# Expert blocks of a transformer kernel: VectorE's products ahead of the move of the last result, TensorE's turning of the products in two halves

## Chip, cores, metric

The kernel runs on one core of a Trainium2 chip (trn2) in one launch. The metric is device time in microseconds, the median of several runs.

## What is computed

A block of 512 tokens of width 1024 passes through a first layer (a parallel mixer, cross attention and a mixture of experts) and two further layers (a token mixer with four branches, a norm, a mixture of experts, a norm). All in float32. The change is in the mixture of experts, which occurs three times. Cut to what matters:

```python
# 4 groups x 8 experts; top-1 group, then the top-2 experts in it
expert_id = g_idx * EXPERTS_PER_GROUP + e_local            # (T, 2)
weights = p_top * softmax(e_top)
# rows are sorted by expert and padded to blocks; each block has one expert e
def expert_block(xb, e):
    return (silu(xb @ w_gate[e]) * (xb @ w_up[e])) @ w_down[e]
out[t] += w_sorted[t] * y_disp[dest]                       # two contributions a token
```

The first mixture has gate and up matrices of 1024x512 an expert, the second and third of 1024x256. There are 32 experts in each, and 1024 pairs of token and expert.

## The kernel before

`program` calls its stages one after the other, with a barrier of all engines between them. Three calls of `moe` are the expert stages; their tiles have the prefix `e_` in the profile. I call them first (FF = 512), second and third stage (FF = 256).

**Work and tiles.** In `moe` the tokens of each expert are cut into blocks of SLOTS = 64 rows, so that most experts have one block and a few have two or more (some 35 blocks a stage). Gate and up weights lie in a ring of RING places (3 in the first stage, 6 in the others), down weights in another. SyncE fills both at the start; then `refill` loads expert e + RING into a place as soon as the gate and up matmuls of expert e are through (`gu_ready`), and its down weights as soon as its down matmuls are (`y_ready`).

**One block g, by engine.** Every engine has its own loop over experts and their blocks, and counts them in a register `done`. What happens in it is in the order of the code:

- GpSimd gathers the rows of block g + 3 from DRAM into `landing` (`gather`), when `stage_rows` has emptied it. Then it waits for VectorE's `move_y` of block g's result (`y_moved`) and stores `y_out` to DRAM by an indirect DMA (L1223). Both go through the queue for software-made DMAs, with two small operations ahead of each issue (`tokcur` or `choicecur`, and `aside`).
- VectorE: `move_y(g)` copies block g - 1's result from `y` to `y_out` (L1162). It waits for ScalarE's copy to `y` (`y_copied`) and for the store before the last (`y_stored`), which has to have left `y_out`. Then, for each half q, the product of silu(gate) and up into `hid` (L1170); `turn_copy(g + 2)` copies the turned rows of the next block to `xT` (L1140, L1142); `stage_rows(g + 2)` waits for the gather and copies `landing` to `gathered` (L1147).
- TensorE: 2 x 8 pairs of gate and up matmuls, half by half (L997, L999); `turn`, which turns the gathered rows of the next block with the identity matrix (L976, L978); the turning of the products, half 0 and half 1, each after `hid_ready` (L1009); the down matmuls (L1020), which wait for ScalarE's copies `hidT` and for `y_copied`.
- ScalarE: two silus (L1048), two copies of the turned products to `hidT` (L1051), then the copy of the result to `y` (L1055), which waits for `y_moved`: `y` may be overwritten once the last result has been moved.

The waits around the move, in the code:

```python
                def move_y(n):
                    dve.wait_ge(y_copied, n + 1)
                    dve.wait_ge(y_stored, n * 16 + 16)
                    vec.tensor_copy(y_out[:], y[:]).then_inc(y_moved, 1)
```

Before the loops, GpSimd issues two spare stores (L1204), so that `y_stored` is already 32 for the first moves, and gathers 0, 1 and 2. VectorE scales `x` before its first `stage_rows` in the second and third stage (L1151). After the loops VectorE moves the last result; SyncE reads all results back when every store has landed (L941), and VectorE adds them to `x` (L1181).

## Time and profile before

| | us |
|---|---|
| median of 3 runs | 3223.39 |
| lowest, highest | 3221.16, 3237.9 |
| the profiled execution | 3233.42 |
| its span, first to last instruction | 3231.7 |
| busy: TensorE / VectorE / ScalarE / GpSimd | 2530.7 / 1255.3 / 944.7 / 364.4 |
| granted TensorE clock, mean | 0.879 |

How to read the profile. Times are counted from the start of the span. PE is TensorE (PEld its weight loads), DVE VectorE, ACT ScalarE, POOL GpSimd, SP SyncE; a q behind a name is that engine's sequencer. A group or an instruction is named by its line in the kernel, engine, operation, and written tile <- read tiles. In brackets or behind a bar stands the idle time of the engine just before it, and what ended it. A granted clock of 1 is 2.4 GHz and 0.5 is 1.2 GHz. An indirect DMA's row on GpSimd is its issue, not its transfer. The share of DMA is the mean busy share of the core's 16 DMA engines.

### The profile page before, as it was taken

What the parts mean: (1) busy time and instruction counts of PE and PEld (TensorE: products, weight loads), DVE (VectorE), ACT (ScalarE), POOL (GpSimd) and SP (SyncE); (2) the same over time, 40 slices, a digit from 0 to 9 for tenths busy, and PEclk for the clock granted to TensorE, in tenths of its full rate; (3) what the DMA queues carried; (4) which work ended last, traced back from release to release, by engine and by line L of the source; (5) the groups of instructions that cost most, each with busy time, mean ns of one, the idle gap of its engine ahead of it and who ended that gap; (6) DMA issues with size and microseconds to landing.
All of it is one profiled execution on the core that took longest, in us unless ns stands there. A gap on an engine that the chain in (4) does not pass through costs nothing. (4 is left out here: it accounts for less than half of the span.)

```text
span 3231.7 us, 51558 instructions
## 1 busy us (share of the span) xinstructions
PE 2530.7 (78%) x17988; PEld 1959.7 (61%) x17989; DVE 1255.3 (39%) x2672; ACT 944.7 (29%) x1720; POOL 364.4 (11%) x706
## 2 busy tenths in 40 slices
PE   4974698589889859699898388894969998658883
PEld 4963688445445438476677266663847677636662
DVE  3447334311111145447443432235734753432224
ACT  2233323112112122236322133332234532213232
POOL 0000000012111110000000233231000000113233
PEclk9987899789999979799999598896979999768887
DMA  3201231489999942122121669944122121289972
GB/s 119 80 1 39 66 117 53 181 354 407 414 409 412 404 153 75 33 66 66 50 57 56 276 234 348 349 182 139 53 57 58 49 63 44 65 347 363 362 298 100
DMA packets 208903, 565.75 MB, mean 175 GB/s; under 512 B 26198, under 2 KB 170198, under 8 KB 184192
## 3 DMA queue, kind: packets, MB, share of 16 engines
q1 hardware_dynamic: 191056, 538.71, 45.1%
q0 software_dynamic: 17712, 25.23, 2.4%
q8 instruction: 86, 1.41, 0.2%
q14 instruction: 49, 0.40, 0.0%
HBM read 560.18 MB, written 35.92 MB: 184 GB/s over the span
## 5 line engine op out<-in xcount | busy, mean ns | idle before, releaser
L997 PE MATMUL ps<-e_wgu,e_xT 128*64 128x128 f32 (+1 forms) x2688 | 426.4, 321 | 41.2 <-issue 22.5
L997 PEld LDWEIGHTS ps<-e_wgu,e_xT 128*64 128x64 f32 x2688 | 344.4, 147 | 165.2 <-issue 116.7
L999 PE MATMUL ps<-e_wgu,e_xT 128*64 128x128 f32 (+1 forms) x2688 | 426.1, 321 | 0.0
L999 PEld LDWEIGHTS ps<-e_wgu,e_xT 128*64 128x64 f32 x2688 | 344.0, 147 | 0.0
L1020 PE MATMUL ps<-e_wd,e_hidT 128*64 128x512 f32 x1112 | 303.8, 682 | 5.4 <-ACT e_hidT L1051 4.0
L1903 PE MATMUL ps<-t_hT,t0a_t0g_w 128*128 128x512 f32 x768 | 199.2, 411 | 4.6 <-DVE t0a_t0g_w L1925 2.4
L1903 PE MATMUL ps<-t_hT,t1a_t1g_w 128*128 128x512 f32 x768 | 198.0, 409 | 4.6 <-DVE t1a_t1g_w L1925 2.4
L1162 DVE COPY e_y_out<-e_y 128x512 f32<-128x512 f32 x108 | 46.3, 429 | 372.9 <-DMA e_dram_y<-e_y_out,e_choicecur 267.4
L447 POOL TENSOR_TENSOR all_x<-all_x,ln_rows 128x1024 f32<-128x1024 f32 x16 | 48.2, 3040 | 1262.5 <-DVE all_x L440 1262.5
L1170 DVE TENSOR_TENSOR e_hid<-e_silu,ps 64x128 f32<-64x128 f32 (+1 forms) x210 | 67.1, 334 | 299.5 <-ACT e_silu L1048 293.0
L1048 ACT ACTIVATE e_silu<-ps 64x128 f32<-64x128 f32 (+1 forms) x210 | 63.9, 304 | 378.5 <-PE ps L999 377.5
L1903 PEld LDWEIGHTS ps<-t_hT,t0a_t0g_w 128*128 128x128 f32 x768 | 145.4, 194 | 45.7 <-issue 10.3
L1903 PEld LDWEIGHTS ps<-t_hT,t1a_t1g_w 128*128 128x128 f32 x768 | 144.5, 193 | 45.4 <-issue 10.3
L1147 DVE COPY e_gathered<-e_landing 64x1024 f32<-64x1024 f32 x111 | 76.3, 687 | 229.4 <-DMA e_landing<-e_dram_rows,e_tokcur 228.1
L1020 PEld LDWEIGHTS ps<-e_wd,e_hidT 128*64 128x64 f32 x1112 | 82.5, 151 | 127.7 <-issue 107.7
L1048 ACT ACT_TABLE_LOAD x105 | 134.7, 1283 | 76.3 <-issue 70.0
L1009 PE MATMUL ps<-all_ident,e_hid 64*128 64x64 f32 x556 | 101.2, 308 | 65.8 <-DVE e_hid L1170 64.2
L1055 ACT COPY e_y<-ps 128x512 f32<-128x512 f32 x105 | 61.6, 586 | 280.8 <-PE ps L1020 278.9
L1009 PEld LDWEIGHTS ps<-all_ident,e_hid 64*128 64x128 f32 x556 | 82.1, 204 | 74.1 <-DVE e_hid L1170 73.3
L1199 POOL DMA_INDIRECT e_landing<-e_dram_rows,e_tokcur x114 | 112.9, 990 | 58.8 <-issue 54.2
L1223 POOL DMA_INDIRECT e_dram_y<-e_y_out,e_choicecur x105 | 109.4, 1042 | 57.1 <-issue 57.1
L1051 ACT COPY e_hidT<-ps 128x64 f32<-128x64 f32 (+1 forms) x210 | 48.1, 230 | 173.6 <-PE ps L1009 168.6
(604 smaller groups left out, 4738.6 us busy)
## 6 DMA issues: line engine op xcount, KB each, us to landing
e_wgu<-in_w_exp_gate_up SPq DMA_DIRECT2D x54, 2048.0 KB, 9.2
e_wgu<-in_w_gate_up SPq DMA_DIRECT2D x22, 4096.0 KB
e_wd<-in_w_down SPq DMA_DIRECT2D x32, 2048.0 KB
e_wd<-in_w_exp_down SPq DMA_DIRECT2D x64, 1024.0 KB
m_both<-in_w_gate_up SPq DMA_DIRECT2D x10, 4096.0 KB, 37.8
r_hT<-in_w_exp_gate_up SPq DMA_DIRECT2D x10, 2048.0 KB
t0a_t0g_raw<-in_w_in SPq DMA_DIRECT2D x32, 512.0 KB
t1a_t1g_raw<-in_w_in SPq DMA_DIRECT2D x32, 512.0 KB
```

The source lines that it names most:

```text
L447: nc.gpsimd.tensor_tensor(x[:, t, :], x[:, t, :], rows[:, 1], ALU.add).then_inc(shifted, 1)
L997: nc.tensor.matmul(ps_gu[q][0:SLOTS], xT[:, c, :], wgu[s][:, 0, c, span], start=c == 0, stop=c == DC - 1)
L999: last = nc.tensor.matmul(ps_gu[q][SLOTS:P], xT[:, c, :], wgu[s][:, 1, c, span], start=c == 0, stop=c == DC - 1)
L1009: last = nc.tensor.matmul(ps_hid[q][:, f * SLOTS:(f + 1) * SLOTS], hid[SLOTS:P, q, f * P:(f + 1) * P], ident[SLOTS:P, SLOTS:P], start=True ...
L1020: last = nc.tensor.matmul(ps_y[h * SLOTS:(h + 1) * SLOTS], hidT[:, f, :], wd[s][:, f, h * 512:(h + 1) * 512], start=f == 0, stop=f == NF - 1)
L1048: nc.scalar.activation(silu[SLOTS:P, q], ps_gu[q][0:SLOTS], ACT.Silu).then_inc(silu_ready, 1)
L1055: nc.scalar.copy(y[:], ps_y).then_inc(y_copied, 1)
L1147: vec.tensor_copy(gathered[:], landing[:]).then_inc(rows_staged, 1)
L1170: vec.tensor_tensor(hid[SLOTS:P, q], silu[SLOTS:P, q], ps_gu[q][SLOTS:P], ALU.mult).then_inc(hid_ready, 1)
L1199: nc.gpsimd.indirect_dma_start(landing[:], None, rows_dram, bass.IndirectOffsetOnAxis(tokcur[:], 0), bounds_check=S - 1, oob_is_err=False) ...
L1223: nc.gpsimd.indirect_dma_start(y_dram, bass.IndirectOffsetOnAxis(choicecur[:], 0), y_out[:], None, bounds_check=4 * S - 1, oob_is_err=Fals ...
L1903: last = nc.tensor.matmul(ps[:, 6, :], w[:, p, q, :], self.hT[:, r, q, :], start=q == 0 and p == r, stop=q == DC - 1 and p == LO)
```

## The change

VectorE's loop makes the two products of a block first, then copies the turned rows, and moves the last result behind that, ahead of the copy of the next rows. TensorE turns the first half of the products right behind the gate and up matmuls, then the next rows, then the second half. Before the loops, GpSimd issues the first gather ahead of the two spare stores.

```diff
--- before.py
+++ after.py
@@ -979,6 +979,15 @@
                                                    ident[0:SLOTS, 0:SLOTS])
                     last.then_inc(turned, 1)
 
+                def turn_hid(g, q):
+
+                    pe.wait_ge(hid_ready, g * 2 + (q + 1))
+                    for f in range(HF):
+                        last = nc.tensor.matmul(ps_hid[q][:, f * SLOTS:(f + 1) * SLOTS],
+                                                hid[SLOTS:P, q, f * P:(f + 1) * P], ident[SLOTS:P, SLOTS:P],
+                                                start=True, stop=True)
+                    last.then_inc(hid_turned, 1)
+
                 pe.wait_ge(rows_staged, 1)
                 turn()
                 done = pe.alloc_register(f"{name}_done")
@@ -1000,16 +1009,10 @@
                                                         start=c == 0, stop=c == DC - 1)
                             last.then_inc(gu_ready, 1)
 
+                        turn_hid(g, 0)
                         pe.wait_ge(rows_staged, g + 2)
                         turn()
-                        for q in range(2):
-                            pe.wait_ge(hid_ready, g * 2 + (q + 1))
-                            for f in range(HF):
-
-                                last = nc.tensor.matmul(ps_hid[q][:, f * SLOTS:(f + 1) * SLOTS],
-                                                        hid[SLOTS:P, q, f * P:(f + 1) * P], ident[SLOTS:P, SLOTS:P],
-                                                        start=True, stop=True)
-                            last.then_inc(hid_turned, 1)
+                        turn_hid(g, 1)
 
                         pe.wait_ge(w_sem[s][1], (turn_ + 1) * 16)
                         pe.wait_ge(y_copied, g + 1)
@@ -1164,11 +1167,11 @@
                 with dve.Fori(0, NE) as e:
                     with dve.Fori(0, blocks_of(dve, e)):
                         g = dve.snap(done)
-                        move_y(g)
                         for q in range(2):
                             dve.wait_ge(silu_ready, g * 2 + (q + 1))
                             vec.tensor_tensor(hid[SLOTS:P, q], silu[SLOTS:P, q], ps_gu[q][SLOTS:P], ALU.mult).then_inc(hid_ready, 1)
                         turn_copy(g + 2)
+                        move_y(g)
                         stage_rows(g + 2)
                         dve.reg_add(done, done, 1)
                 move_y(dve.snap(done))
@@ -1200,10 +1203,10 @@
                                                  bounds_check=S - 1, oob_is_err=False).then_inc(rows_gathered, 16)
 
 
+                pool.wait_ge(landing_cleared, 1)
+                gather(0)
                 for n in range(2):
                     nc.gpsimd.dma_start(spare_dram[n:n + 1], ident[0:1, 0:SLOTS]).then_inc(y_stored, 16)
-                pool.wait_ge(landing_cleared, 1)
-                gather(0)
                 for n in (1, 2):
                     pool.wait_ge(rows_staged, n)
                     gather(n)
```

VectorE, the body of the loop over blocks in the first stage (`y_out<-y` is the move, `hid` the products, `xT` the copy of the turned rows, `gathered<-landing` the copy of the next rows; ISA and REGISTER_ALU are waits and counts). Before:

```order
L1162 COPY e_y_out<-e_y 128x512
L1169 ISA
L1170 TENSOR_TENSOR e_hid<-e_silu,ps 64x256
L1169 REGISTER_ALU
L1170 TENSOR_TENSOR e_hid<-e_silu,ps 64x256
L1137 REGISTER_ALU
L1142 TENSOR_TENSOR e_xT<-ps,all_columns 128x512
L1146 ISA
L1147 COPY e_gathered<-e_landing 64x1024
```

And in the changed kernel:

```order
L1172 TENSOR_TENSOR e_hid<-e_silu,ps 64x256
L1171 REGISTER_ALU
L1172 TENSOR_TENSOR e_hid<-e_silu,ps 64x256
L1140 REGISTER_ALU
L1145 TENSOR_TENSOR e_xT<-ps,all_columns 128x512
L1163 REGISTER_ALU
L1164 ISA
L1165 COPY e_y_out<-e_y 128x512
L1149 ISA
L1150 COPY e_gathered<-e_landing 64x1024
```

The move went from the first place, ahead of both products, to the one between the copy of the turned rows and the copy of the gathered rows.

GpSimd, ahead of its loop in the first stage, before (`spare` are the spare stores, `landing` the gather with its two small operations):

```order
L1204 DMA e_dram_spare<-all_ident 16x1x4 x2
L1196 COPY e_tokcur<-e_tokcol 64x1
L1188 TENSOR_TENSOR e_aside<-all_ident 1x1
L1199 DMA e_landing<-e_dram_rows,e_tokcur 64x1024
L1196 COPY e_tokcur<-e_tokcol 64x1
```

And in the changed kernel:

```order
L1199 COPY e_tokcur<-e_tokcol 64x1
L1191 TENSOR_TENSOR e_aside<-all_ident 1x1
L1202 DMA e_landing<-e_dram_rows,e_tokcur 64x1024
L1209 DMA e_dram_spare<-all_ident 16x1x4 x2
L1199 COPY e_tokcur<-e_tokcol 64x1
```

The first gather with its two operations went ahead of the two spare stores, which now stand before the second gather.

## Rows read from the trace of the kernel before

**Rows 1.** Windows: us, engines' busy time, TensorE's granted clock, DMA share, GB/s
```profile
700.00:1100.00 400.00, 347.94 (x2574) 202.17 (x2572) 69.32 (x133) 84.25 (x159) 74.16 (x162) 0.94 1.01 409
1940.00:2020.00 80.00, 66.92 (x731) 49.93 (x729) 20.66 (x44) 23.71 (x53) 25.92 (x54) 0.87 0.92 353
2930.00:3000.00 70.00, 59.01 (x627) 44.28 (x625) 16.64 (x36) 21.27 (x44) 20.55 (x45) 0.85 0.98 369
2148.00:2184.00 36.00, 33.51 (x427) 25.45 (x425) 12.03 (x26) 14.76 (x31) 14.37 (x33) 1.00 0.05 14
```

**Rows 2.** Waits in 1845:2148 (two rows), 2870:3182 (three): total, times, longest
```profile
DVE e_y_out L1162 <- DMA e_dram_y<-e_y_out,e_choicecur: 99.5, 21, 7.7
PE ps L1009 <- DVE e_hid L1170: 28.0, 17, 3.5
...
DVE e_y_out L1162 <- DMA e_dram_y<-e_y_out,e_choicecur: 102.7, 24, 6.3
DVE e_gathered L1147 <- DMA e_landing<-e_dram_rows,e_tokcur: 83.4, 28, 9.1
PE ps L1009 <- DVE e_hid L1170: 32.4, 23, 3.1
```

**Rows 3.** VectorE in order of time, third stage: start, duration, what [idle before]
```profile
2936.74 0.43 DVE L1162 COPY e_y_out<-e_y 128x512 f32<-128x512 f32 x1 [6.30 <-DMA e_dram_y<-e_y_out,e_choicecur]
2937.20 0.50 DVE L1170 TENSOR_TENSOR e_hid<-e_silu,ps 64x128 f32<-64x128 f32 x2
...
2939.63 0.69 DVE L1147 COPY e_gathered<-e_landing 64x1024 f32<-64x1024 f32 x1 [1.22 <-DMA e_landing<-e_dram_rows,e_tokcur]
2945.17 0.43 DVE L1162 COPY e_y_out<-e_y 128x512 f32<-128x512 f32 x1 [4.85 <-DMA e_dram_y<-e_y_out,e_choicecur]
```

**Rows 4.** GpSimd in order of time, the same place: the issue of a store
```profile
2938.57 1.03 POOL L1223 DMA_INDIRECT e_dram_y<-e_y_out,e_choicecur  x1 [0.54 <-issue]
```

**Rows 5.** VectorE: moves that wait for a store where a loaded stretch ends
```profile
1877.40 0.43 DVE L1162 COPY e_y_out<-e_y 128x512 f32<-128x512 f32 x1 [7.74 <-DMA e_dram_y<-e_y_out,e_choicecur]
...
2143.64 0.43 DVE L1162 COPY e_y_out<-e_y 128x512 f32<-128x512 f32 x1 [5.83 <-DMA e_dram_y<-e_y_out,e_choicecur]
2144.10 0.29 DVE L1170 TENSOR_TENSOR e_hid<-e_silu,ps 64x128 f32<-64x128 f32 x1
...
2151.17 0.29 DVE L1170 TENSOR_TENSOR e_hid<-e_silu,ps 64x128 f32<-64x128 f32 x1 [1.58 <-ACT e_silu L1048]
...
3086.63 0.43 DVE L1162 COPY e_y_out<-e_y 128x512 f32<-128x512 f32 x1 [5.04 <-DMA e_dram_y<-e_y_out,e_choicecur]
```

**Rows 6.** VectorE where a loaded stretch begins, second stage
```profile
1897.47 0.68 DVE L1147 COPY e_gathered<-e_landing 64x1024 f32<-64x1024 f32 x1 [2.27 <-DMA e_landing<-e_dram_rows,e_tokcur]
1898.97 0.43 DVE L1162 COPY e_y_out<-e_y 128x512 f32<-128x512 f32 x1 [0.82 <-DMA e_dram_y<-e_y_out,e_choicecur]
```

**Rows 7.** The end of the third stage in order of time
```profile
3177.69 0.69 DVE L1140 COPY e_xT<-ps 128x512 f32<-128x512 f32 x1
...
3180.77 0.43 DVE L1162 COPY e_y_out<-e_y 128x512 f32<-128x512 f32 x1 [1.68 <-ACT e_y L1055]
...
3182.60 1.03 POOL L1223 DMA_INDIRECT e_dram_y<-e_y_out,e_choicecur  x1 [0.54 <-issue]
3184.96 3.80 SPq L941 DMA_DIRECT2D e_wgu<-e_dram_y  x8
```

**Rows 8.** The start of a stage: GpSimd's spare stores, VectorE's scaling of x
```profile
645.16 1.28 POOL L1204 DMA_DIRECT2D e_dram_spare<-all_ident  x2 [636.40 <-DVE e_tokcol L1134]
...
1838.46 2.27 DVE L1151 TENSOR_SCALAR all_x<-all_x 128x4096 f32<-128x4096 f32 x1
1839.16 2.20 POOL L1204 DMA_DIRECT2D e_dram_spare<-all_ident  x2 [41.71 <-DVE e_tokcol L1134]
```

**Rows 9.** GpSimd: a store issue that met the copy, and the gather's behind it
```profile
1953.92 1.47 POOL L1223 DMA_INDIRECT e_dram_y<-e_y_out,e_choicecur  x1 [0.54 <-issue]
...
1956.38 0.98 POOL L1199 DMA_INDIRECT e_landing<-e_dram_rows,e_tokcur  x1 [0.51 <-issue]
```

## The prediction

> **What bounds the kernel now.** The change is inside the three expert stages, so I read those first: the stretches for what each is short of, then the waits of VectorE and TensorE in each, then the order of time around one wait. I call the stages first (665 to 1165 us, 512 columns), second (1845 to 2184) and third (2885 to 3182; both 256 columns). The reader should see three regimes. In the first stage the transfers' share is 1.01 from 700 to 1100 us; in the loaded parts of the second and third it is 0.92 and 0.98; and the last blocks of the second run with 0.05 and TensorE at the full clock [rows 1]. So the first stage waits for weights, and a faster block buys nothing there beyond its first and last blocks. In the other two, TensorE is behind the weights: each ends with a run of blocks for which nothing is being loaded.
>
> What holds TensorE back there? VectorE's move of the last result waits for the store before it 21 times in the second stage and 24 times in the third, 99.5 and 102.7 us together, and TensorE waits 28.0 and 32.4 us for the products [rows 2]. The two belong together: in the order of time a move starts 6.30 us late, the products (0.50 us) begin the moment it ends, and the next move waits 4.85 us again [rows 3]. The products' own operands had been ready, since both follow without a gap. TensorE is thus made to wait for a store that its block does not need.
>
> But the wait is a loop of its own. A move (0.43 us) releases GpSimd, whose store issue ends at 2939.60, 2.43 us after the move's end at 2937.17, and the store lands 5.6 us later, when the next move starts at 2945.17: 8.43 us from move to move [rows 3, 4]. The gather has a like loop: the copy of the rows (0.69 us) releases GpSimd for the next gather, and the next copy waits for that one; VectorE waits for gathers 28 times in the third stage, 83.4 us [rows 2, 3]. TensorE is in neither loop. Taking the products out from behind the move does not shorten them.
>
> **The change, part by part.** No instruction is added or removed.
>
> (1) *Products ahead of the move.* In a loaded stretch the products no longer wait for the store but for the copy of the rows before them, which ends 5 us or so sooner. TensorE gets ahead once, by at most the wait plus the 0.46 us of the move; the pace stays that of the loops. The lead becomes time only where a loaded stretch ends and the following block is held by TensorE. I find four such places, three in the second stage and one in the third, by moves that wait over 4 us for a store and are followed by a block whose products wait for ScalarE; the first (7.74 us) and the last (5.04 us) stand in [rows 5]. The one at 2143.64, worked out: the product after it is at 2151.17, held by ScalarE's silu, so by TensorE. Now the copy of the rows follows the move at 2144.10, ends at 2144.8, and after 0.77 us of loop overhead (the gap that stays before a move when its store has all but landed, 0.82 us [rows 6]) the products can start at 2145.6: 5.6 us sooner [rows 5]. Bounds for one place: nothing (the loops start late again) and 8.2 us (7.74 + 0.46). I take 4.0, below the worked one because TensorE's own 7 us a block (2144.10 to 2151.17) can come last: 4 x 4.0 = **-16.0 us**, 12 of it in the second stage.
>
> (2) *The move behind the turned copy.* In a block paced by TensorE the move used to wait for ScalarE and now stands some 4 us later, right before the copy of the rows. GpSimd therefore has store and gather to issue in one piece. If a gather goes out as long after its copy as a store after its move, its issue used to end 0.69 + 2.43 = 3.12 us after the turned copy. Now the store's ends after 0.03 + 0.43 + 2.43 = 2.89 us, and a gather right behind a store ends 1.97 us later (1955.39 to 1957.36 [rows 9]), so at 4.86: 1.7 us later. Where a loaded stretch begins with a wait for the gather, as the 2.27 us at 1897.47 [rows 6], the products behind it come later. Bounds 0 and 1.7 us; I take 1.2, since the overhead and the move that stood between copy and products are partly saved. There are four such entries, three in the second stage and one in the third: 4 x 1.2 = **+4.8 us**.
>
> (3) *The last two moves.* The last block but one's result is now moved after the last turned copy, which ends at 3178.38; its store issue ends 2.89 us later at 3181.27. An issue ended at 3183.63 and the read back began at 3184.96, so an unloaded store takes 1.33 us [rows 7]. It lands at 3182.6, and the last move, at 3180.77 before, waits for it, 1.8 us; GpSimd, busy until 3183.2 with the last gather, adds 0.1: **+1.9 us** for each of the two narrow stages, 3.8 together. In the wide one the down matmuls are twice as long, and they cover it; if that cover were gone it would be 1.9 more. Lower bound: nothing.
>
> (4) *The first gather ahead of two spare stores.* The spares took 2.20 us of GpSimd before the second stage's first gather and 1.28 before the first's [rows 8]. TensorE waits for this gather with its weights loaded. First stage: -1.3. In the others the first spare ran beside VectorE's scaling of x (2.27 us, until 1840.73), and a pair took 1.28 us without it and 2.20 with it, so a part of those 2.20 us is not the spares' own. The gather now runs in that place. Bounds 0 and 2.2; I take 0.6 each, as if GpSimd's work could finish only when the scaling does. Sum **-2.5 us**. The Trainium skill, "SBUF — State Buffer", section "SBUF: two separate sides", states that a DVE copy of fp32 from SBUF to SBUF locks GpSimd out so that it cannot write descriptors; the spares' 2.20 us beside the scaling agree. By that rule the gather gains nearly nothing there; without it, 2.2 us.
>
> (5) *The second place for contention on GpSimd.* A store issue that met the copy of the rows took 1.47 us [rows 9] where others take 1.03 [rows 4]. Now the copy follows the move at once and ends 0.72 us after it, while the issue starts 1.40 us after it (2937.17 to 2938.57): they miss each other unless the copy waits for its gather. Zero, bounds -0.4 and +0.4 us a block; in blocks paced by TensorE, GpSimd's idle time covers it. The same page's rule speaks against a move and a copy in one piece, since both are such copies; by it the issue would be late in every block.
>
> (6) *Turning in two halves.* The first half goes ahead of the rows, the second behind. The down matmuls need both, and the second product waits for ScalarE and so for TensorE's gate and up matmuls either way. Zero; bounds -0.3 and +0.3 us for the few blocks paced by TensorE. Cover: the second silu and product. What is now queued behind the wait for the first product is the turning of the next rows; if the products are late, so is the copy of the turned rows, with the down matmuls as its cover.
>
> Sum: -16.0 + 4.8 + 3.8 - 2.5 = **-9.9 us**. The profiled execution took 3233.4 us (span 3231.7), 10.0 us above the median of 3223.39; I apply the difference to the median: **3213.5 us**. A measurement of this kernel can tell about 0.5%, or 16 us, from no change, so my sum lies inside it.
>
> **The rivals.** *The loops eat everything* (A). The leads of (1) are lost because move and copy restart their loops no sooner. For it: both loops wait for transfers in nearly every loaded block [rows 2]. Against: the tail blocks, where nothing is loaded. Then (2), (3) and (4) remain and nearly cancel, with -2.5 + 3.8 = +1.3 and entries unpaid: 3224.7.
>
> *The wait really goes* (B). The share of 0.92 in the second stage leaves room, and if TensorE gets ahead everywhere, its 28.0 us of waiting for products there vanish, with (4) on top: 3223.4 - 28.0 - 2.5 = 3193. The third stage, at 0.98, has no such room; that is against 60 us.
>
> *The gather becomes the bound* (C), slower. Store ahead of gather in GpSimd's order costs the gather 1.7 us in every block whose next step it decides, not just at entries. It turns the sign from 6 such blocks on (9.9 over 1.7). With half of the third stage's 28 gather waits it is 14 x 1.7 = 24 us, less the 9.9: 3237.5. A second way to it is the 0.4 us of (5) in each of the 45 blocks whose move waits for a store (21 and 24 [rows 2]): 18 us, so 3231.5, 0.03 of C's chance. For it: copies wait for gathers as often as moves for stores. Against: a gather that follows its store closely has been in time before, with 1.22 us of waiting [rows 3].
>
> *The change does nothing in a loaded block* because products wait for the copy of the rows instead is within A.
>
> **How the numbers follow.** Forecast 0.47 (own range 3204 to 3222; a third of it is beyond 16 us, since one or two more places bring it there), A 0.21, B 0.21, C 0.11. Faster by over 0.5%: 0.16 + 0.21, less a little of B, gives 0.36. Slower: C's larger part, 0.08. Same: 0.56. The range that leaves out a part of C and the far end of B is 3190 to 3231.
>
> **What would show it.** Right: TensorE's waits for the products fall from 60 us to under 25; the moves still wait for stores some 100 us in each narrow stage; the last move of a narrow stage waits about 2 us for a store; the first gather starts 1.3 us sooner in the first stage; the second stage shortens by about 9 us, the first and third by 1 to 3. Wrong: loaded blocks with another period than 8.4 to 10 us, either way, or VectorE's wait for gathers well above the 83.4 us of the third stage.

## The result and the profile after

| | before | after |
|---|---|---|
| median, same chip | 3227.66 us (19 runs) | 3243.95 us (19 runs) |
| lowest, highest | 3219.38, 3246.53 | 3235.53, 3250.7 |
| span of the profiled execution | 3231.7 | 3248.3 |
| first stage, first copy of the rows to last move | 503.8 | 505.6 |
| second stage | 333.5 | 342.1 |
| third stage | 302.8 | 311.1 |

The ratio is 1.0048 (95% interval 1.0035 to 1.0061): slower, by about 16 us, where the forecast was 9.9 us faster; the range, too, ended below it. The loss is in the two narrow stages, +8.6 and +8.3 us; the stage lengths come from VectorE's order of time, of one profiled execution each. Such a length has its own scatter: two profiled executions of one kernel further down have 322.5 and 316.3 us in the second stage, 298.3 and 298.2 in the third.

Windows of the changed kernel, with the columns of [rows 1]:

```profile
700.00:1100.00 400.00, 341.74 (x2562) 192.63 (x2560) 68.20 (x132) 83.66 (x158) 73.80 (x159) 0.93 1.01 407
...
2930.00:3000.00 70.00, 50.25 (x553) 35.29 (x555) 16.28 (x35) 18.84 (x42) 19.46 (x43) 0.83 0.95 355
```

The first stage is where it was. In the third the transfers move 355 GB/s instead of 369, and every engine is busy less [rows 1]. Waits of the changed kernel, second stage (two rows), then the third (two rows):

```profile
DVE e_gathered L1150 <- DMA e_landing<-e_dram_rows,e_tokcur: 148.3, 33, 9.3
PE ps L986 <- DVE e_hid L1172: 53.7, 27, 4.3
...
DVE e_gathered L1150 <- DMA e_landing<-e_dram_rows,e_tokcur: 153.4, 32, 8.6
PE ps L986 <- DVE e_hid L1172: 59.7, 19, 5.6
```

The wait for the store, 99.5 and 102.7 us before [rows 2], has all but left the list: it is 16 us (7 times) and 9 us (3 times). The wait for the gather stands in its place: 153.4 us in the third stage instead of 83.4. And TensorE, for which the products were put first, waits longer for them: 113.4 us in the two stages instead of 60.4. VectorE and GpSimd in order of time, third stage, loaded blocks of the changed kernel:

```profile
2960.67 0.69 DVE L1150 COPY e_gathered<-e_landing 64x1024 f32<-64x1024 f32 x1 [5.08 <-DMA e_landing<-e_dram_rows,e_tokcur]
2962.05 0.50 DVE L1172 TENSOR_TENSOR e_hid<-e_silu,ps 64x128 f32<-64x128 f32 x2 [0.69 <-ACT e_silu L1051]
2963.39 0.69 DVE L1143 COPY e_xT<-ps 128x512 f32<-128x512 f32 x1 [0.85 <-PE ps L978]
2964.12 0.43 DVE L1165 COPY e_y_out<-e_y 128x512 f32<-128x512 f32 x1
2971.78 0.69 DVE L1150 COPY e_gathered<-e_landing 64x1024 f32<-64x1024 f32 x1 [7.24 <-DMA e_landing<-e_dram_rows,e_tokcur]
2973.16 0.50 DVE L1172 TENSOR_TENSOR e_hid<-e_silu,ps 64x128 f32<-64x128 f32 x2 [0.69 <-issue]
2975.06 0.69 DVE L1143 COPY e_xT<-ps 128x512 f32<-128x512 f32 x1 [1.40 <-PE ps L978]
2975.78 0.43 DVE L1165 COPY e_y_out<-e_y 128x512 f32<-128x512 f32 x1
2980.52 0.69 DVE L1150 COPY e_gathered<-e_landing 64x1024 f32<-64x1024 f32 x1 [4.31 <-DMA e_landing<-e_dram_rows,e_tokcur]
```

```profile
2962.72 0.99 POOL L1202 DMA_INDIRECT e_landing<-e_dram_rows,e_tokcur  x1 [0.51 <-issue]
...
2965.93 1.03 POOL L1226 DMA_INDIRECT e_dram_y<-e_y_out,e_choicecur  x1 [0.55 <-issue]
...
2973.83 0.99 POOL L1202 DMA_INDIRECT e_landing<-e_dram_rows,e_tokcur  x1 [0.51 <-issue]
```

Before, VectorE waited twice a block, 4.85 us for the store and 1.22 us for the gather [rows 3]. Now it waits once, in front of the copy of the rows, and products, turned copy and move follow with no longer wait than 1.40 us between them. The loop that is left is the gather's: copy 0.69 us, 1.36 us until GpSimd starts the issue (2961.36 to 2962.72), issue 0.99 us, and a flight of 8.07 us to the next copy (2963.71 to 2971.78), then one of 5.70 us. The store goes out 3.2 us behind the gather, in the gather's flight.

Where the copy of the rows finds its gather landed, it is the other way round. The move stands right ahead of the copy, so GpSimd has the store first and the gather behind it; here the copy, which had not waited, ended at 2918.99:

```profile
2919.86 1.03 POOL L1226 DMA_INDIRECT e_dram_y<-e_y_out,e_choicecur  x1 [0.56 <-issue]
...
2922.14 0.99 POOL L1202 DMA_INDIRECT e_landing<-e_dram_rows,e_tokcur  x1 [0.51 <-issue]
```

The gather is issued 3.15 us behind the copy instead of 1.36. The next copy waits for it, 11.7 us behind this one.

**Words used from here on.** A *loaded block* is one whose copy of the rows starts over 7.5 us after the one before it; there are 26 to 28 in each narrow stage of both kernels. Its *spacing* is that distance. A *flight* runs from the end of an issue on GpSimd to the start of the VectorE copy or move that waited for it. In the loaded blocks that waited for a gather:

| kernel | gather-waited of loaded (2nd, 3rd) | mean flight | mean spacing of all loaded blocks |
|---|---|---|---|
| before | 17 of 27, 25 of 28 | 6.68, 6.49 | 9.54, 9.35 |
| after | 26 of 27, 26 of 26 | 6.67, 6.85 | 9.75, 10.01 |

The limit of 7.5 us chooses these blocks. Without it, the mean distance from copy to copy over the whole stage is 8.49 and 8.84 us before, 8.67 and 9.03 after. In the unloaded blocks the median distance from the copy's end to the next gather's issue is 1.36 us before in both stages, and 2.7 and 3.1 us after.

### The profile page after: what moved, and what is told of

The parts are those of the page before. It is cut to its first block and busy times, and to the rows that moved or that the text cites. A ratio compares the mean times of both kernels' runs of the same rounds, so it can differ in the third digit from the quotient of the medians.

```text
span 3248.3 us, 51561 instructions
## 1 busy us (share of the span) xinstructions
PE 2504.8 (77%) x17988; PEld 1925.3 (59%) x17989; DVE 1252.5 (39%) x2672; ACT 943.6 (29%) x1720; POOL 370.6 (11%) x706
## 3 DMA queue, kind: packets, MB, share of 16 engines
q0 software_dynamic: 17712, 25.23, 2.4%
## 5 line engine op out<-in xcount | busy, mean ns | idle before, releaser
L1006 PE MATMUL ps<-e_wgu,e_xT 128*64 128x128 f32 (+1 forms) x2688 | 420.4, 318 | 42.5 <-DMA e_wgu<-in_w_gate_up 32.9
L1006 PEld LDWEIGHTS ps<-e_wgu,e_xT 128*64 128x64 f32 x2688 | 338.6, 145 | 168.0 <-issue 118.6
L1008 PE MATMUL ps<-e_wgu,e_xT 128*64 128x128 f32 (+1 forms) x2688 | 420.4, 318 | 0.0
L1008 PEld LDWEIGHTS ps<-e_wgu,e_xT 128*64 128x64 f32 x2688 | 338.4, 145 | 0.0
L986 PE MATMUL ps<-all_ident,e_hid 64*128 64x64 f32 x556 | 115.7, 311 | 122.7 <-DVE e_hid L1172 117.2
L986 PEld LDWEIGHTS ps<-all_ident,e_hid 64*128 64x128 f32 x556 | 85.0, 203 | 157.1 <-DVE e_hid L1172 139.3
L1199 POOL COPY e_tokcur<-e_tokcol 64x1 uint32 (+1 forms) x114 | 24.2, 212 | 1049.6 <-DVE e_tokcol L1137 716.8
L1226 POOL DMA_INDIRECT e_dram_y<-e_y_out,e_choicecur x105 | 110.7, 1054 | 55.8 <-issue 55.8
```

The source lines that it names most:

```text
L986: last = nc.tensor.matmul(ps_hid[q][:, f * SLOTS:(f + 1) * SLOTS], hid[SLOTS:P, q, f * P:(f + 1) * P], ident[SLOTS:P, SLOTS:P], start=True ...
L1006: nc.tensor.matmul(ps_gu[q][0:SLOTS], xT[:, c, :], wgu[s][:, 0, c, span], start=c == 0, stop=c == DC - 1)
L1008: last = nc.tensor.matmul(ps_gu[q][SLOTS:P], xT[:, c, :], wgu[s][:, 1, c, span], start=c == 0, stop=c == DC - 1)
L1226: nc.gpsimd.indirect_dma_start(y_dram, bass.IndirectOffsetOnAxis(choicecur[:], 0), y_out[:], None, bounds_check=4 * S - 1, oob_is_err=Fals ...
```

## The experiments

I began with two theories. **Theory 1**: VectorE's new order makes the gather's loop lead at every loaded block, the store goes out in its flight, and that pace is slower. **Theory 2**: TensorE's new order costs, since the rows are turned later and the turned copy waits for them (48.0 us in the two narrow stages of the changed kernel, 5.9 before). Every ratio below is to the kernel before on the same chip, with a 95% interval; stage lengths, flights and spacings are of the one profiled execution.

### The change taken apart

Four kernels, each with a part of the diff shown above: VectorE's order alone (dve_only), TensorE's halves alone (pe_only), the first gather ahead of the spares alone (gather_first), and the whole change with the move between the products and the turned copy (move_second; its edit against the changed kernel):

```diff
+                        move_y(g)
                         turn_copy(g + 2)
-                        move_y(g)
                         stage_rows(g + 2)
```

> VectorE's new order alone; TensorE turns the rows and then both halves as before, the spare stores stay first. Theory 1 (the copy of the rows and its gather now lead, each store goes out in the gather's flight, and the gathers land later): slower than before by 10 to 20 us, stages two and three each 6 to 10 us longer, as in the whole change. Theory 2 (what costs is TensorE's new order: the turning of the next rows is queued behind the wait for the products, and with it the turned copy, the move and the next copy of rows): -5 to +3 us against before.

> TensorE's turning in two halves alone; VectorE moves first, as before, the spare stores stay first. Theory 1: within 4 us of before. Theory 2: slower by 8 us or more, since the first product still waits for the move and now the turning of the rows waits with it.

> The first gather ahead of the spare stores alone. Both theories: 1 to 4 us faster than before, too little to be told for certain; the first stage's first copy of rows 2 us sooner, the others' within 1 us.

> The whole change, but the move stands between the products and the turned copy, in the time in which VectorE waits 1.4 us for the turned rows. The store goes out some 2 us sooner after the gather's issue (2 instead of 4 us behind). Theory 1: if only the lead of the gather matters, as slow as the change (+12 to +20 us against before); if the store's place in the gather's flight matters too, it moves by more than 4 us from the change, either way. Theory 2: 0 to +8 us against before, since nothing of the move is left between the turned copy and the copy of the rows.

| kernel | median, us | ratio | second, third stage, us |
|---|---|---|---|
| dve_only | 3251.46 | 1.0071 (1.0047 to 1.0096) | 338.2, 311.5 |
| pe_only | 3221.23 | 0.9988 (0.9971 to 1.0005) | 327.6, 296.5 |
| gather_first | 3230.36 | 1.0006 (0.9988 to 1.0023) | 336.4, 308.0 |
| move_second | 3231.52 | 1.0017 (1.0005 to 1.0030) | 331.5, 306.4 |

The wait for the gather in the third stage, VectorE's order alone, with the waits for the store and TensorE's for the copied rows; below, the same stage with TensorE's halves alone (both from 2885 us on):

```profile
DVE e_gathered L1147 <- DMA e_landing<-e_dram_rows,e_tokcur: 170.6, 29, 9.3
DVE e_y_out L1162 <- DMA e_dram_y<-e_y_out,e_choicecur: 7.8, 3, 3.7
PE ps L976 <- DVE e_gathered L1147: 54.7, 17, 13.5
```

```profile
DVE e_y_out L1165 <- DMA e_dram_y<-e_y_out,e_choicecur: 106.1, 23, 7.5
PE ps L986 <- DVE e_hid L1173: 47.7, 22, 4.2
DVE e_gathered L1150 <- DMA e_landing<-e_dram_rows,e_tokcur: 41.5, 22, 6.6
```

VectorE's order alone gives the whole loss (1.0071; its interval overlaps that of the whole change); theory 2 falls. TensorE's halves alone change the time by nothing that can be measured. They only rename a stop: with VectorE's order and the old TensorE order, TensorE stands 54.7 us in the third stage at the turning of the gathered rows (L976), with the halves 59.7 us at the products (L986) that now come first. Both stand behind VectorE's wait for the gather. The move one place earlier costs about a third of the full change. The store then goes out 0.6 and 1.6 us sooner in the gather's flight (medians of the two narrow stages), and where a store stands ahead of the gather of a loaded block, that gather is up to 1.0 us late and not up to 1.8. The run does not tell these two apart. The profiled execution with the first gather alone, which acts once a stage, had most loaded blocks under the gather's lead as well (in the third stage 143 us of waiting for gathers, 50 for stores). It was the slowest of the 12 runs of its kernel, 3238.53 us, while their median is no different from before: which loop leads in the old order hangs on little, and the profile need not be the typical run.

### A little more delay, a little less

Four small GpSimd operations go ahead of the gather's issue or of the store's (after_gather_late, after_store_late; `aside` made wider for them):

```diff
                     pool.wait_ge(tokcur_ready, n + 1)
                     step_aside()
+                    nc.gpsimd.tensor_tensor(aside[:, 1:2], ident[0:1, 0:1], ident[0:1, 0:1], ALU.mult)
...
```

And the other way: the copy of the next row numbers is made when the gather has landed, beside VectorE's copy of the rows, in the changed kernel (after_pick_early) and with TensorE's half alone (pe_pick_early):

```diff
+                def pick(n):
+                    pool.wait_ge(rows_gathered, n * 16)
+                    nc.gpsimd.tensor_copy(tokcur[:], tokcol[:, bass.ds(n, 1)]).then_inc(tokcur_ready, 1)
...
+                        pick(g + 3)
                         pool.wait_ge(rows_staged, g + 3)
                         gather(g + 3)
```

> The changed kernel with four more small GpSimd operations (0.26 us each by the spacing of such operations in the profile after, so 1.04 us) between the copy of the rows and the gather's issue; nothing left out. Theory 1 (the gather's loop leads in the changed kernel: copy, 1.4 us on GpSimd, issue, some 7 us of landing, copy): each of the 65 blocks of the second and third stage at which the copy waits for the gather grows by 1.0 us, so 45 to 70 us more than the changed kernel, some 3290 to 3312 us. Theory 3 (the pace is set by the weights that fill the DMA engines, and the wait for the gather only shows that): the added microsecond is taken out of the wait, and the time stays within 10 us of the changed kernel's 3244.

> The changed kernel with the same four small operations (1.04 us) ahead of the store's issue instead of the gather's; nothing left out. Theory 1: the store has slack in the changed kernel (the move waits for it at 10 of 65 blocks only), so most of the delay is absorbed: 0 to 15 us more than the changed kernel, far less than with the gather delayed. If the store, going out 3.2 us behind the gather, lengthens the gather's landing, a store at 4.2 us changes the landing by some tenths of a microsecond either way, up to 20 us. Theory 3: within 10 us. The opposite of theory 1 (the store's loop leads after all): 45 to 70 us more.

> The changed kernel with GpSimd's copy of the next row numbers made as soon as the gather before has landed, beside VectorE's 0.69 us copy of the rows, instead of behind it; nothing left out. It takes 0.26 us out of the gather's loop. Theory 1: 65 blocks by 0.26 us, so 12 to 20 us less than the changed kernel (about 3226 to 3232), and less still if the first stage's waits count. Theory 3: no change within 5 us.

> TensorE's half of the change alone (VectorE's and GpSimd's order as before the change), with the same 0.26 us taken out of the gather's loop. In this order the store's loop and the gather's loop lead about equally often. Theory 1: 25 gathers and 48 stores are waited for, so 0.26 us goes at the gathers alone, and the store's loop takes part of it: 0 to 7 us less than the 3221 us of TensorE's half alone, thus 3214 to 3221, which would be faster than both kernels. Theory 3: 3221 within 4 us.

| kernel | median, us | ratio |
|---|---|---|
| after_gather_late | 3250.83 | 1.0065 (1.0044 to 1.0085) |
| after_store_late | 3249.75 | 1.0062 (1.0036 to 1.0087) |
| after_pick_early | 3236.03 | 1.0022 (1.0008 to 1.0036) |
| pe_pick_early | 3220.22 | 0.9963 (0.9946 to 0.9980) |

My sizes were wrong twice. The four operations follow each other every 0.145 us, and the last ones run in the 0.51 us that the issue takes to begin anyway, so the issue came 0.23 us later and not 1.04:

```profile
2955.95 0.18 POOL L1199 COPY e_tokcur<-e_tokcol 64x1 uint32 x1 [2.90 <-DVE e_gathered L1150]
...
2956.79 0.18 POOL L1205 TENSOR_TENSOR e_aside<-all_ident 1x1 f32<-1x1 f32 x1
2957.12 0.99 POOL L1206 DMA_INDIRECT e_landing<-e_dram_rows,e_tokcur  x1 [0.15 <-issue]
```

The delay runs therefore say nothing of theory 1 in size: 0.23 us by 65 blocks is 15 us, and 1.0065 against 1.0048 is 5 us, with overlapping intervals; the store delayed as much gives the same, 1.0062. The early copy took out more than I said, 0.49 us (0.87 instead of 1.36 from copy to issue), which by a fixed flight is 32 us for 65 blocks; the time fell by 1.0048 less 1.0022, or 8 us. The flight explains most of the rest: in the loaded blocks it grew from 6.67 and 6.85 to 7.19 and 7.21 us, and their spacing was 10.24 and 9.93. A gather that left sooner arrived hardly sooner. Besides, the gathers of nine of the 48 loaded blocks were issued behind a store and left no sooner at all. (The two stages as a whole were shorter, 335.9 and 302.8 us: there were fewer loaded blocks, 48 instead of 53.) With TensorE's halves alone the early copy gives 0.9963 for 0.9988, 8 us, also with overlapping intervals.

### Two microseconds more

Sixteen operations instead of four, in both kernels, ahead of the gather's or of the store's issue. The distance from copy to issue grew from 1.36 to 3.32 us: 1.96, as meant. Theory 3 is that only the weights' bytes count; theory 4, formed on the runs above, says that the gather leads but that most of its flight is a wait behind queued weight packets, and so no constant.

> The changed kernel with sixteen more small GpSimd operations ahead of the gather's issue; by the run with four of them, where they follow each other every 0.145 us and cover 0.36 us of the issue's own preparation, they put the issue 1.96 us later. Nothing left out. Theory 1 (gather leads, its landing takes a fixed time): 65 blocks by 1.96 us, 127 us more than the changed kernel, some 3370 us. Theory 4 (the gather leads, but its landing is mostly a wait behind queued weight packets; a later block frees weight buffers later, so the queue is shorter when the gather comes, and part of the delay is given back): by the run with four operations, 6 us for 65 times 0.22 us, about 0.4 of the delay shows, so 50 us (30 to 80), and the mean flight of a waited-for gather falls from 6.0 us to under 5.2 us. Theory 3 (only the weights' bytes count): under 15 us.

> The changed kernel with the same sixteen operations (1.96 us) ahead of the store's issue; nothing left out. The store goes out 3.3 us behind the gather and has some 2 us of slack before its landing holds up the move. Theories 1 and 4: half of the blocks or fewer pay, and a part of 1.96 us each, so 10 to 50 us more than the changed kernel, less than with the gather delayed. If the store led, it would be over 80 us.

> The kernel before the change with the sixteen operations (1.96 us) ahead of the gather's issue; nothing left out. The gather's and the store's loop lead at about 50 and 45 blocks of the two narrow stages. Delaying the gather makes it lead nearly everywhere. Theory 1: 90 to 120 us more than before. Theory 4: 0.4 of that, 30 to 60 us, and the mean flight falls below 5.5 us.

> The kernel before the change with the sixteen operations (1.96 us) ahead of the store's issue; nothing left out. Theory 1: the store, which in this order is moved right behind the copy of the rows, leads nearly everywhere, 90 to 120 us more than before, and more than the changed kernel loses by the same delay of its store. Theory 4: 30 to 60 us more, and again more than the changed kernel loses, because in the old order the store's loop holds up the products and through them TensorE. If the order of VectorE didn't matter for which loop leads, the store's delay would cost the same in both kernels.

| kernel | median, us | ratio | over its own order, us | mean flight in loaded blocks, 2nd, 3rd |
|---|---|---|---|---|
| after_gather_2us | 3311.56 | 1.0283 (1.0251 to 1.0316) | 76 | 5.03, 5.46 |
| after_store_2us | 3293.01 | 1.0217 (1.0180 to 1.0254) | 54 | 6.44, 6.52 |
| before_gather_2us | 3330.66 | 1.0344 (1.0307 to 1.0382) | 111 | 5.10, 5.05 |
| before_store_2us | 3270.22 | 1.0153 (1.0121 to 1.0185) | 49 | 5.80, 6.10 |

("Over its own order" is the ratio less 1.0048, or less 1, times 3227.66. The flights without a delay are 6.67 and 6.85 in the changed kernel, 6.68 and 6.49 before.) Theory 3 falls. The gather delayed by 1.96 us costs 76 us in the changed kernel, not the 127 of a fixed flight; in the profiles the two narrow stages have 18.0 and 16.0 of it. In loaded blocks the flight is 1.4 to 1.6 us shorter in both kernels: well over half of the delay is given back there. That is what theory 4 asked for. (Over all waited-for gathers the mean falls further, to 4.2 and 4.6 us, but partly because all 75 copies now wait, the unloaded ones too.)

Three sizes miss. The gather delayed in the old order costs 111 us, where theory 4 had 30 to 60 and theory 1 90 to 120: by the time alone it is theory 1's number, though the flights (5.10 and 5.05 us) are not those of a fixed flight. In its profile the first stage has 23.9 us of it and the narrow ones 38.8 and 28.5; no run explains why it pays more than the changed kernel. Delaying the store costs the changed kernel 54 us where I had 10 to 50, and the old one 49 where I had more than the changed kernel. It does not follow that the store leads. In the changed kernel the delayed store's issue holds up the next gather on GpSimd: the median distance from copy to gather issue, over all blocks, rose from 1.37 to over 3.2 us in these profiles. So the store's delay does not tell the orders apart, and my expectation that it would was wrong.

### Without most of the weights

Refills of a ring place load only the first quarter:

```diff
-                                     w_gate_up[bass.ds(e, 1)].rearrange("e p m c f -> p (e m c f)")).then_inc(w_sem[s][0], 16)
+                                     w_gate_up[bass.ds(e, 1)].rearrange("e p m c f -> p (e m c f)")[:, 0:2 * DC * FF // part]).then_inc(w_sem[s][0], 16)
```

(with `part` = 4 in `refill`, and the same for down).

> The kernel before the change with every refill of a weight buffer loading only the first quarter of its elements (the first loads of each ring are whole): three quarters of the refilled weights are left out, so the output isn't the reference's. Theory 4 (the flight of gather and store is mostly a wait behind queued weight packets): the flight falls from 6 us to the 1.8 to 2.9 us seen where no weights move, and the narrow stages fall from 333 and 303 us to 200 to 260. Theory 1 (a fixed flight of 6 to 7 us): the loops keep their 9.3 us and the narrow stages shorten by under 10%.

> The changed kernel with the same quarter refills (output not the reference's). Theory 4: the loss comes from where the two small transfers stand among the weight packets, so it is gone here: within 0.3% of before_light or faster by up to 1%, as products made first serve TensorE sooner. Theory 5 (the new order costs by itself, through the instructions that stand ahead of the store's issue on VectorE and GpSimd): still slower than before_light by 10 us or more.

> VectorE's new order alone on the old TensorE order, with the same quarter refills (output not the reference's). Theory 4: like after_light, within 0.4% of before_light on either side; theory 5: slower than before_light by 10 us or more, as VectorE's order alone was 23 us slower with whole refills.

Medians 3002.54, 2998.63 and 3009.27 us; ratios to the kernel before 0.9315 (0.9291 to 0.9340), 0.9303 (0.9279 to 0.9328) and 0.9335 (0.9310 to 0.9360). Windows 2700 to 2900 us, before_light, then after_light:

```profile
2700.00:2900.00 200.00, 189.02 (x2381) 150.72 (x2381) 67.22 (x142) 77.09 (x165) 76.98 (x168) 0.96 0.47 151
```

```profile
2700.00:2900.00 200.00, 188.38 (x2433) 147.52 (x2435) 68.55 (x143) 79.24 (x168) 83.33 (x171) 0.96 0.49 158
```

The narrow stages are 244.1 and 251.6 us in the old order, 248.3 and 246.1 in the new one: TensorE paces both. (The wrong outputs send the tokens of the next layers to other experts; the narrow stages have 37 and 38 copies of rows instead of 40 and 35, the same sum.) The mean flight of the waited-for gathers is 3.6 and 3.1 us in after_light, where the changed kernel has 5.9 and 6.1, so little more than half, though not the 1.8 to 2.9 I had expected. And the loss is gone: the new order is 3.9 us faster than the old, inside the intervals. VectorE's order alone is 6.7 us slower, also inside; with whole refills it was 23 us. So the weights' traffic is needed for the loss. The runs do not say by which of its effects: with quarter refills TensorE paces the stages, and the loops of VectorE no longer do.

### Without the store's bytes

The store is issued and waited for, but its row limit lets no row but the first through; what is read back comes from the gathered rows' source.

```diff
-                                                     bounds_check=4 * S - 1, oob_is_err=False).then_inc(y_stored, 16)
+                                                     bounds_check=0, oob_is_err=False).then_inc(y_stored, 16)
```

> The kernel before the change with the store's row limit set to 0, so that it is issued and waited for as before but writes no row beyond the first; the read back takes the gathered rows' source instead. The results of the experts are left out of the output. Theory 4a (the store's packets share the queue with the gather's and lengthen its flight, in the new order at every loaded block): both kernels get faster, and the new order by more, so that the difference of 16 us shrinks to under 5. Theory 4b (the flight depends on the weights' queue and on when the gather comes alone): the difference stays above 10 us. In this order the store's loop no longer leads if its landing gets short.

> The changed kernel with the same two edits (results of the experts left out of the output). Theory 4a: within 5 us of before_nostore or faster, and the mean spacing of the copies in the loaded blocks of the last narrow stage falls from 10.0 to 9.4 us or less. Theory 4b: over 10 us slower than before_nostore, spacing still near 10 us.

Medians 3207.88 and 3217.16 us; ratios 0.9939 (0.9915 to 0.9963) and 0.9969 (0.9949 to 0.9989). Waits from 2885 us on (the third stage begins at 2853 and 2852 here), old order, then new:

```profile
DVE e_y_out L1162 <- DMA e_dram_y<-e_y_out,e_choicecur: 90.5, 22, 6.1
DVE e_gathered L1147 <- DMA e_landing<-e_dram_rows,e_tokcur: 60.8, 26, 6.6
```

```profile
DVE e_gathered L1150 <- DMA e_landing<-e_dram_rows,e_tokcur: 111.9, 26, 7.2
...
DVE e_y_out L1165 <- DMA e_dram_y<-e_y_out,e_choicecur: 14.0, 6, 3.3
```

A store that moves almost nothing is waited for nearly as long as a full one, 90.5 us against 102.7 [rows 2], so its bytes are not what its flight consists of. Its packets stay, though: the profile's page counts 17712 packets in the software queue with and without the bytes (12.68 MB instead of 25.23). The difference of the orders is 9.3 us by the medians, between my two marks, and the intervals of the two ratios overlap. The new order gained 0.8% and the old 0.6%, so a part of the loss may hang on the bytes; the spacing of the loaded blocks stays apart, 9.29 in the third stage of the old order and 9.79 in the new. Theory 4a, that the store's packets lengthen the gather's flight in the new order, is not settled by this, since only the bytes were taken out; 4b fits the spacing, while the medians alone are too near each other to say.

### A version faster than both

> TensorE's half of the change and the earlier copy of the row numbers, run again: 0.9963 of before in its first run, so 0.994 to 0.998 again; if that was chance, 1.000.

Run again, TensorE's halves with the early copy of the row numbers took 3212.46 us, ratio 0.9968 (0.9953 to 0.9983); the first time it was 0.9963. That is 10 to 12 us less than before and 26 to 27 less than the changed kernel. Its move waits for stores 120.6 us in the third stage and its copy for gathers 22.0 from 2885 us on (42.5 in the whole stage, 83.4 before [rows 2]):

```profile
DVE e_y_out L1165 <- DMA e_dram_y<-e_y_out,e_choicecur: 120.6, 23, 7.0
DVE e_gathered L1150 <- DMA e_landing<-e_dram_rows,e_tokcur: 22.0, 8, 5.8
```

It waits longer for its stores than the kernel before, and it is faster. The loaded blocks are 8.83 and 9.22 us apart.

## Why the prediction was wrong

The sign was wrong. The step that failed is in part (1): "the pace stays that of the loops". I had both loops in hand, with 8.43 us from move to move, and took them for fixed and independent, so that taking the products out from behind the move could only help TensorE. The new order does not leave them as they were. With the move behind the copy that waits for the gather, the store seldom leads; 52 of 53 loaded blocks wait for the gather instead of 42 of 55, and the blocks are 9.75 and 10.01 us apart instead of 9.54 and 9.35. The 8.6 and 8.3 us of the two narrow stages can be split by the profiles. The last move, counted from the last copy, is 1.6 us of each (term 3). Late gathers ahead of loaded blocks are at most 3.0 and 3.6 (term 2). What remains, 4.0 and 3.1 us, stands where -12 and -4 were forecast.

- **(1) Products ahead of the move**, -16.0: the step that failed. VectorE's order alone, which holds terms 1 to 3 and by my sum should gain 7.4 us, measured about +23 us (15 to 31). The products did leave the store's wait, and got the gather's instead, since they stand behind the copy of the rows. I had seen that ("the products no longer wait for the store but for the copy of the rows") and reckoned the copy 5 us sooner, which holds for one block and not for a loop: the next gather starts from that same copy.
- **(2) Later gathers**, +4.8: right in mechanism and number, and a little small. At four blocks (two in each narrow stage, not three and one) the store's issue stands ahead of the gather for which the next, loaded block waits. That issue starts 2.87, 2.86, 3.15 and 3.13 us behind the end of the copy instead of 1.36, so 1.5 to 1.8 us late where I took 1.2, 6.6 us in all. In the other loaded blocks the gather's issue stands ahead of the store's (2962.72 and 2965.93). In the profiles of the kernel before, of TensorE's halves alone and of the first gather alone no gather for which a loaded block waits is late in this way.
- **(3) The last two moves**, +1.9 each: right. From the last product to the last move it was 3.4 us in the third stage before, and is 5.7 in the rows below; in the second it went from 3.4 to 5.3. So +2.3 and +1.9.

```profile
3192.40 0.29 DVE L1172 TENSOR_TENSOR e_hid<-e_silu,ps 64x128 f32<-64x128 f32 x1 [0.61 <-ACT e_silu L1051]
...
3198.07 0.43 DVE L1165 COPY e_y_out<-e_y 128x512 f32<-128x512 f32 x1 [3.26 <-DMA e_dram_y<-e_y_out,e_choicecur]
```

- **(4) The first gather**, -2.5: right, as far as its own step goes. The first stage's first copy came 2.1 us sooner (657.8 for 659.9), 1.6 of it after the row numbers were ready, where I had 1.3. In the other two, counted from the start of VectorE's scaling, the gather's issue started 0.8 us sooner and the first copy 0.3 and 0.5 us sooner, where I had 0.6. The Trainium skill ("SBUF — State Buffer", "SBUF: two separate sides") states that GpSimd is locked out while VectorE runs an operation that takes both ports, such as an fp32 copy within SBUF. The trace agrees for the scaling: GpSimd's copy of the row numbers, 0.2 us elsewhere, took 2.01 us beside it and ended with it. But the gather gained more than the next to nothing that I had worked out by that rule, since the rest of the spares' work used to follow the scaling. The whole first stage was no shorter for it, and the first gather alone made no measurable difference (1.0006).
- **(5) Contention on GpSimd**, zero: right. A store's issue took 1054 ns on average, 1042 before.
- **(6) TensorE's halves**, zero: 0.9988 with an interval that holds 1. But the reason given was incomplete: TensorE waits for products far more with it, 49.5 us in the third stage against 32.4 [rows 2], and loses nothing by it. In its profile the narrow stages were even shorter (327.6 and 296.5 us), more than my bounds allow; the medians don't confirm that as a gain.

Of the rivals, C was on the right side, and "VectorE's wait for gathers well above the 83.4 us" was named as what would prove me wrong. Its trigger, a store ahead of the gather on GpSimd at 1.7 us each, is there in the unloaded blocks and delays the gather of four loaded ones, too few to turn the sign by the 6 that I had reckoned; in the other loaded blocks the gather became the bound without it. Its chance of 0.11 was too low, because I counted a gather that had waited 1.22 us as one that is in time.

**What stays open.** It is shown that VectorE's order causes the loss, that the gather then leads, that its flight falls to little more than half with a quarter of the weights, and that the loss needs those weights. It is not shown how the loss is shared out. No run keeps the store behind the gather on GpSimd in the new order, so what the late gathers cost is only read from the profile; by the same reading they come to some 9 us with VectorE's order alone, 6.6 in the changed kernel and 5 with the move second, which is the order of the three ratios. Nor is it shown why the other gather-led blocks are longer than mixed ones. The store's bytes are at most a part of it. What is left is argument: in the old order the two small transfers hang on two separate waits, each of which hides the other's, while in the new one everything hangs on one landing; TensorE then frees the weight buffers in a less even rhythm, and the transfers idle more (0.95 for 0.98). The copies do come less evenly: loaded blocks of the third stage are 8.1 to 12.5 us apart, long and short by turns, where they were 7.8 to 10.9. A second landing buffer would test it; it was not tried.

## What to carry to other kernels

A wait in a profile belongs to a loop. Before moving it, write down every loop that closes through the same queue and engine, with its period, and ask which leads once this one is free; where both are waited for in most blocks, as here, most of the removed wait comes back at the other: VectorE waited 177 us less for stores in the narrow stages and 140 us more for gathers. And a small transfer's flight beside full weight traffic is no constant: in this kernel it shrank when issued later and grew when issued sooner, so an edit to the issue was worth less than its own length. An operation moved on one engine can also turn round the order of issues on another: look at the blocks that wait for nothing, too. Total waiting is no measure of a version: the fastest kernel here that leaves nothing out waits longer for its stores than the one before.

## What the runs showed of the hardware that was not expected

- The flight of an indirect gather of 64 rows is set by the other traffic: 6.5 to 6.9 us on average in loaded blocks, 3.1 to 3.6 us over a narrow stage with a quarter of the refills, about 2 us in the last, unloaded blocks (2.01 and 1.82 among them). A store that writes almost nothing, with the same number of packets, is waited for nearly as long as one that writes all its rows (90.5 and 102.7 us over the third stage).
- A copy of 64 numbers on GpSimd, 0.2 us elsewhere, took 2.01 us beside VectorE's scaling of 2.28 us and ended with it, in both narrow stages.
- Small GpSimd operations (0.18 us each) follow each other every 0.145 us, and up to 0.36 us of them vanish in the time that an indirect DMA takes to start anyway: four of them delayed the issue by 0.23 us, sixteen by 1.96.
